# Two batches inside the fourth query slot and a router on the turned residual

## The chip, the cores and the metric

The kernel runs on one core of a Trainium2 chip. The metric is the device time of one execution in microseconds; less is better. Times are compared between medians of several executions.

## What is computed

The reference runs two model blocks over 256 tokens of width 1024, all in float32. The first block has two layers. Each mixes the tokens (a gated linear recurrence in layer 0, stick-breaking attention in layer 1), then looks up rows of a large table (PEER), then adds a gated embedding:

```python
h = h + peer_ffn(rms_norm(h, norm_ffn[i]), peer_w_q[i], peer_sub_keys[i], peer_u[i], peer_v[i])
```

The lookup has 8 heads. For each token and head, 16 of 16,384 rows are picked by two sets of 128 sub-keys; a row of `peer_u` is multiplied with the token, the product goes through gelu and a gate, and scales a row of `peer_v` that is added up. The second block mixes the tokens once more (dilated attention and a chunked recurrence), adds the normed result, and runs a mixture of 32 experts, of which each token uses 4:

```python
x = x + gate_m[:, None, :] * rms_norm_2(y, g_post_mix[l])
h = modulate(rms_norm_2(x, g_pre_ffn[l]), shift_f, scale_f)   # norm * g * (1 + scale) + shift
logits = h @ w_router + b_router
top_val, top_idx = lax.top_k(logits, 4)
gates = jax.nn.softmax(top_val, axis=-1)
act = x_glu * sigmoid(1.702 * x_glu) * (x_lin + 1.0)          # x_glu, x_lin = h @ w_gu[e] + b_gu[e], clipped at 7
y = act @ w_down[e] + b_down[e]
```

## The kernel before

**Layout.** The tokens stand in two tiles of 128 (`t` is 0 or 1). `h` is the residual, `hs` a normed copy, `xT` the turned copy in which the features are on the partitions. PSUM has eight banks: 0 to 2 rotate for projections, 3 is spare, 4 to 7 hold turned tiles, lookup sums or expert outputs. Engines synchronise by counting semaphores, and each engine's instruction stream is written out by hand, in order.

**Lookup layer** (`peer(l, i)` on each engine). The query projection comes in four slots of 512 features. For each slot TensorE projects four quarters (`features`, line 526), ScalarE copies them (line 1189), TensorE multiplies with the sub-keys (line 690), and ScalarE copies the scores (line 1196). VectorE finds the best 16 of each head (`topk`). A pick is one gather on GpSimd's queue (line 2132): 128 rows, one for each token of the tile, each 1024 values of u and 1024 of v, into one of 12 row buffers. There are 256 picks per layer. VectorE multiplies the u half with the token and sums (line 1708). After four picks (a batch) ScalarE applies gelu (line 1154), VectorE the gate (line 1723), ScalarE makes four diagonal matrices (line 1160), and TensorE multiplies them with the v halves into PSUM (`mix_rows`, line 637). Only then, by the semaphore `v_done`, may a new gather overwrite the row buffers. `row_plan` says which buffer each pick uses: eight rotate at first, since four hold the weights of query slots 2 and 3; two join at pick 24 and two at pick 40. Batches 0 and 4 are mixed between the quarters of slot 2, batch 8 behind slot 2's keys, batch 12 behind the second quarter of slot 3, and batch 16 and all later ones behind slot 3. In ScalarE's order the copy of slot 3's first tile stands ahead of batch 12.

**From the output projection to the experts.** `mix_out` is projected in four tiles (lines 541 and 1365 to 1370). VectorE forms the normed, gated result and adds it to `h` (line 1979), squares the residual for its norm, scales it (`scaled`, line 1444), and TensorE turns it (`turn(8, ysb)`, line 557). ScalarE (tile 0) and VectorE (tile 1) copy the turned tile with gain and shift into `xT`. TensorE multiplies with the router's weights `wr`, once for each tile (line 980), and adds the router's bias (line 982). VectorE meanwhile writes the normed rows `hs` with gain (`row_g`) and shift (`row_s`), and clears the buffers `G4`, `Y`, `SGT`, `E` (line 1998). Behind the logits it finds the four best experts of each token (`member`). TensorE counts the tokens of each expert (line 989) and ranks them (991 to 993), and each expert gets blocks of 64 tokens. TensorE gathers the first block's tokens by a one-hot product (`gather`, line 963), turns ranks, gates and rows, and makes tables of experts and ranks for all blocks (lines 1014 to 1020). The product of the gates with the down bias `bdn` starts the output banks 4 to 7 (line 1025).

**Expert loop.** One pass for each block, with a number of passes that is read from memory. A pass starts the gate and up banks with the bias (line 1045), multiplies with eight quarters of weights (line 1051), scatters the block before into the output banks (line 1032), gathers the next block's tokens, and multiplies with four down quarters (line 1077). SyncE loads the weights, 12 MB for an expert, into 12 slots of 1 MB; an expert's first slot is loaded when the last block of the expert before has freed it (`w_free`). GpSimd tells TensorE that a slot's weights are in (`w_here`). After the loop the last block is scattered (line 1032), and the two tiles are normed and stored.

## Time and profile before

| what | value |
|---|---|
| median of 3 runs | 2931.41 us (2931.3 to 2933.35) |
| profiled execution, its own time | 2923.44 us |
| its span, first to last instruction | 2921.3 us |
| busy in the span | TensorE 80%, VectorE 47%, ScalarE 21%, GpSimd 20% |
| mean granted TensorE clock | 0.893 |
| read from HBM | 1047.72 MB, 359 GB/s over the span |

### The profile page before, as it was taken

How to read it: one execution, taken by the hardware profiler on the slowest of the kernel's cores; microseconds unless marked ns; L12 is line 12 of the kernel's file. 1: busy time of each engine (PE TensorE's matmuls, PEld its weight loads, DVE VectorE, ACT ScalarE, POOL GpSimd, SP SyncE). 2: the span in 40 equal slices, each digit the busy share in tenths (PEclk: the TensorE clock that was granted, in tenths of full speed). 3: DMA queues.
4: the chain of work that ended last, by engine and by line, in shares of the span. 5: the costliest groups of instructions: out<-in, count | busy, mean ns of one | idle time of the engine just before them, and what ended most of it. 6: DMA issues, size and time to landing. Idle time of an engine off the chain costs nothing.

```text
span 2921.3 us, 32802 instructions
## 1 busy us (share of the span) xinstructions
PE 2330.0 (80%) x11754; PEld 1004.1 (34%) x11754; DVE 1379.4 (47%) x3401; ACT 604.1 (21%) x1254; POOL 576.7 (20%) x526
## 2 busy tenths in 40 slices
PE   8975556656699975555655699899999999999998
PEld 7741111211165741111211166543333332333333
DVE  5757777776526767777776532521111111111111
ACT  3122212222125112222232121211111111111111
POOL 0034444444300135444444200000000000000000
PEclk9997766887799987777888799889999999999999
DMA  5899999999854899999999743449999999899897
GB/s 220 320 381 422 421 421 421 421 421 421 340 241 159 320 372 419 421 421 421 421 421 418 329 150 116 184 173 387 422 422 422 422 422 422 351 422 422 368 411 293
DMA packets 145310, 1050.19 MB, mean 359 GB/s; under 512 B 16273, under 2 KB 16529, under 8 KB 17969
## 3 DMA queue, kind: packets, MB, share of 16 engines
q0 software_dynamic: 74064, 537.56, 44.6%
q1 hardware_dynamic: 70560, 509.12, 42.7%
q10 hardware_dynamic: 576, 2.16, 0.2%
q8 instruction: 57, 0.93, 0.1%
q14 instruction: 53, 0.43, 0.0%
HBM read 1047.72 MB, written 1.05 MB: 359 GB/s over the span
## 4 chain that ended last, share of the span: by engine, by line
PE 45%; DMA 40%; DVE 5%; POOL 4%; issue 3%; ACT 3%; DVEq 1%; SPq 0%; POOLq 0%
DMA big<-in_peer_uv,rows_of 26%; DMA big<-in_moe 14%; PE psum L1051 11%; PE psum L637 6%; PE psum L526 6%; PE psum L1077 5%; PE psum L541 5%; POOL big L2132 4%; DVE big L1708 2%; PE psum L963 1%; PE psum L1032 1%; PE psum L745 1%; PE psum L654 1%; ACT gdiag L1160 1%; PE psum L1045 1%
## 5 line engine op out<-in xcount | busy, mean ns | idle before, releaser
L637 PE MATMUL psum<-big,gdiag 64*64 64x512 f32 x3728 | 695.3, 847 | 498.2 <-ACT gdiag L1160 498.1
L2132 POOL DMA_INDIRECT big<-in_peer_uv,rows_of x466 | 524.2, 1125 | 1067.9 <-PE psum L637 607.1
L637 PEld LDWEIGHTS psum<-big,gdiag 64*64 64x64 f32 x3728 | 196.0, 189 | 987.2 <-ACT gdiag L1160 603.1
L1051 PE MATMUL psum<-big 128*64 128x512 f32 x2240 | 500.7, 596 | 24.0 <-POOLq L2154 23.3
L1708 DVE CUSTOM_DVE_ANT_0 big<-x_more,big 128x1024 f32<-128x1024 f32 x234 | 286.4, 1226 | 148.9 <-DMA big<-in_peer_uv,rows_of 142.5
L1708 DVE CUSTOM_DVE_ANT_0 big<-mod_rows,big 128x1024 f32<-128x1024 f32 x232 | 284.5, 1227 | 135.1 <-DMA big<-in_peer_uv,rows_of 129.6
L2093 DVE TENSOR_SCALAR big<-psum 128x512 f32<-128x512 f32 x35 | 24.2, 692 | 662.4 <-PE psum L1051 662.4
L1051 PEld LDWEIGHTS psum<-big 128*64 128x64 f32 x2240 | 152.8, 137 | 369.4 <-issue 272.8
L1077 PE MATMUL psum<-ring,big 128*64 128x512 f32 x1120 | 248.0, 594 | 3.7
L1154 ACT ACTIVATE gelu<-dots,rstd 128x4 f32<-128x4 f32 (+1 forms) x134 | 39.8, 297 | 864.8 <-DVE dots L1708 864.7
L526 PE MATMUL psum<-big,ring 128*128 128x256 f32 x832 | 183.3, 380 | 0.8 <-DVE big L1466 0.8
L526 PEld LDWEIGHTS psum<-big,ring 128*128 128x128 f32 x832 | 156.9, 190 | 23.7 <-DVE big L1466 1.2
L541 PE MATMUL psum<-ring,big 128*128 128x512 f32 x352 | 154.2, 595 | 2.7 <-DVE big L1543 1.4
L1160 ACT ACTIVATE gdiag<-small,gated 128x64 f32<-128x64 f32 x512 | 136.9, 336 | 52.9 <-DVE gated L1723 52.1
L1077 PEld LDWEIGHTS psum<-ring,big 128*64 128x64 f32 x1120 | 92.5, 137 | 136.7 <-issue 132.3
L1398 ACT ACTIVATE big<-big 128x512 f32<-128x512 f32 x35 | 22.0, 630 | 487.0 <-DVE big L2093 487.0
L637 PE MATMUL psum<-uv_more,gdiag 64*64 64x512 f32 x368 | 107.3, 709 | 0.0
L541 PEld LDWEIGHTS psum<-ring,big 128*128 128x128 f32 x352 | 66.1, 190 | 83.3 <-issue 78.4
L1032 PE MATMUL psum<-big 64*128 64x512 f32 x288 | 71.5, 615 | 0.7 <-ACT big L1406 0.7
L963 PE MATMUL psum<-big 128*64 128x512 f32 x288 | 71.5, 618 | 0.0
L1406 ACT ACTIVATE big<-psum 128x512 f32<-128x512 f32 x35 | 20.9, 597 | 230.9 <-PE psum L1077 230.9
L1723 DVE SCALAR_TENSOR_TENSOR gated<-gelu,gsum,gexp 128x4 f32<-128x4 f32 (+1 forms) x134 | 29.3, 219 | 67.7 <-ACT gelu L1154 65.3
(394 smaller groups left out, 2142.8 us busy)
## 6 DMA issues: line engine op xcount, KB each, us to landing
big<-in_moe SPq DMA_DIRECT2D x256, 1024.0 KB, 20.1
ring<-in_moe SPq DMA_DIRECT2D x128, 1024.0 KB, 18.9
big<-in_ada SPq DMA_DIRECT2D x24, 1024.0 KB, 11.7
ring<-in_mix_in SPq DMA_DIRECT2D x14, 1024.0 KB, 7.0
ring<-in_a_in SPq DMA_DIRECT2D x8, 1024.0 KB, 8.5
ring<-in_peer_wq SPq DMA_DIRECT2D x8, 1024.0 KB, 7.8
big<-in_peer_wq SPq DMA_DIRECT2D x8, 1024.0 KB, 6.6
ring<-in_ple_gate SPq DMA_DIRECT2D x8, 1024.0 KB, 14.7
```

Of the source, the lines that this page charges most:

```text
L526: mm = pe.matmul(psum[:, (m + t) % 3, f * T:(f + 1) * T], ws[k][:, c:c + P], rhs[:, k, :], start=(k == 0), stop=(k == KC - 1))
L541: mm = pe.matmul(psum[:, (m + t) % 3, :], lhs[:, k, t * P:(t + 1) * P], w[:, k, :], start=(k == 0), stop=(k == KC - 1))
L637: mm = pe.matmul(psum[o:o + HALF, bank, :], gdiag[r:r + HALF, (n + j) % DIAGS, :], v[r:r + HALF, :], start=(at == 0), stop=last, skip_grou ...
L963: mm = pe.matmul(psum[CAP * c:CAP * (c + 1), 2, :], S[:, t, :], hs[:, t, c * 512:(c + 1) * 512], start=(t == 0), stop=(t == TT - 1), skip_ ...
L1032: mm = pe.matmul(psum[:, 4 + 2 * t + c, :], SGT[r, t * P:(t + 1) * P], Y[r, :], start=False, stop=stop, skip_group_check=True)
L1051: mm = pe.matmul(psum[CAP * c:CAP * (c + 1), b, :], xgT[:, k % 4, k // 4, :], wring[k][:, (2 * b + c) * 512:(2 * b + c + 1) * 512], start= ...
L1077: mm = pe.matmul(psum[CAP * c:CAP * (c + 1), 2, :], actT[:, j, f * CAP:(f + 1) * CAP], wring[8 + j][:, (2 * f + c) * 512:(2 * f + c + 1) * ...
L1154: act.activation(gelu[:, cols], dots[:, cols], ACT.Gelu_apprx_tanh, scale=rstd[:, t:t + 1]).then_inc(gelu_ready, 1)
L1160: act.activation(gdiag[:, n % DIAGS, :], ident2, ACT.Copy, scale=gated[:, n:n + 1]).then_inc(gdiag_ready, 1)
L1708: j = dve.tensor_tensor_reduce(out=u, in0=x, in1=u, scale=1.0, scalar=0.0, op0=ALU.mult, op1=ALU.add, accum_out=dots[:, n:n + 1])
L1723: dve.scalar_tensor_tensor(gated[:, cols], gelu[:, cols], total, gexp[:, cols], ALU.mult, ALU.mult).then_inc(gated_act, 1)
L2132: pool.indirect_dma_start(uv[r], None, table, bass.IndirectOffsetOnAxis(rows_of[:, n:n + 1], 0)).then_inc(uv_loaded[r], 16)
```

## The change

Four things are changed.

1. In query slot 3, batch 12 is mixed behind the first quarter and batch 16 behind the third (before: batch 12 behind the second quarter, batch 16 after the slot). ScalarE takes each batch ahead of a tile copy.
2. The router works on the turned residual `h` with the gain only. The inverse root, a factor per token, is applied to the logits afterwards, and the shift's contribution with the router's bias is made once as a row (`logit_bias`). The second tile is turned in two halves, each as soon as its half of `h` is written. The additions of `row_s` are moved: tile 0's ahead of the logits, tile 1's behind `member`.
3. The buffers are cleared before the output projection's tiles come. The output banks are started by `scatter(start=True)`, a product of cleared buffers, behind the logits. The product with `bdn` stands behind the loop, before the last scatter.
4. Order: the first gather stands ahead of the rank turns; gates are formed ahead of the block selection; the register with the number of blocks is loaded earlier on TensorE; the wait for the turned rows stands behind the bias products in the loop; GpSimd signals the first expert's weights before it waits for the table.

```diff
-                inside = {2: {0: 0, 2: BATCH}, 3: {1: 3 * BATCH}}
+                inside = {2: {0: 0, 2: BATCH}, 3: {0: 3 * BATCH, 2: 4 * BATCH}}
...
                     for g in range(2):
+                        if s == 3:
+                            batch((12, 16)[g])
                         act.activation(qT[:, 4 * s + 2 * g:4 * s + 2 * g + 2, :], two(tile_in(m + g)),
                                        ACT.Copy).then_inc(act_took, 1)
...
-                        if s == 3 and g == 0:
-                            batch(12)
...
-            turn(8, ysb)
+            def turn_half(t, b):
+                pe.wait_ge(hs_ready, 17 + t + t * b)
+                for k in range(4):
+                    c = (4 * b + k) * P
+                    mm = pe.transpose(psum[:, 4 + 2 * t + b, k * P:(k + 1) * P], h[:, t, c:c + P], ident)
+                mm.then_inc(turned, 1)
+
+            turn_half(0, 0)
+            turn_half(0, 1)
+            pe.wait_ge(moe_loaded, 160)
+            m = tile0("mix_out") + 1
+            pe.wait_ge(dve_took, TILE_NTH[m])
+            for k in range(KC):
+                pe.matmul(psum[:, m % 3, 0:E2], shift_f[:, k:k + 1].to_broadcast([P, P]), wr[:, k, :],
+                          start=(k == 0), stop=False)
+            pe.matmul(psum[:, m % 3, 0:E2], late[0:1, C_ONES:C_ONES + P], br[0:1, :],
+                      start=False, stop=True).then_inc(row_done, 1)
+            turn_half(1, 0)
+            turn_half(1, 1)
...
             for t in range(TT):
+                pe.wait_ge(xT_ready, 38 + t)
                 if t:
-                    pe.wait_ge(gains_known, 3)
+                    pe.wait_ge(gains_known, 2)
...
+            def scatter(start=False, stop=False):
+                for t in range(TT):
+                    for c in range(2):
+                        r = slice(CAP * c, CAP * (c + 1))
+                        mm = pe.matmul(psum[:, 4 + 2 * t + c, :], SGT[r, t * P:(t + 1) * P], Y[r, :],
+                                       start=start, stop=stop, skip_group_check=True)
+                    if stop:
+                        mm.then_inc(moe_done, 1)
+
+            pe.wait_ge(E_ready, 1)
+            scatter(start=True)
...
             pe.wait_ge(first_ready, 1)
+            gather()
             for t in range(TT):
                 mm = pe.transpose(psum[0:E2, 1, t * P:(t + 1) * P], rank[:, t, :], ident)
             mm.then_inc(rankT_done, 1)
-            gather()
             pe.wait_ge(g_ready, 1)
...
+            n = pe.value_load(blocks[0:1, 0:1], min_val=E2, max_val=BLOCKS - 1)
             turn_rows(1)
...
             with pe.Fori(0, n) as i:
                 pe.wait_ge(E_ready, i + 1)
-                pe.wait_ge(x_taken, i + 1)
                 pe.wait_ge(sgt_taken, i + 1)
...
+                pe.wait_ge(x_taken, i + 1)
                 for k in range(KC):
...
+            for t in range(TT):
+                for c in range(2):
+                    r = slice(E2 * (2 * t + c), E2 * (2 * t + c + 1))
+                    pe.matmul(psum[:, 4 + 2 * t + c, :], gT4[r, :], bdn[r, :], start=False, stop=False,
+                              skip_group_check=True)
             pe.wait_ge(out_taken, n + 1)
-            scatter(True)
+            scatter(stop=True)
```

ScalarE and VectorE at the router, and GpSimd:

```diff
+            def take_half(t, b):
+                act.wait_ge(turned, 32 + 2 * t + b + 1)
                 for k in range(4 * b, 4 * b + 4):
-                    j = act.activation(xT[:, k, 0:P], psum[:, 4 + b, (k % 4) * P:(k % 4 + 1) * P], ACT.Identity,
-                                       scale=gf[:, k:k + 1], bias=shift_f[:, k:k + 1])
+                    j = act.activation(xT[:, k, t * P:(t + 1) * P], psum[:, 4 + 2 * t + b, (k % 4) * P:(k % 4 + 1) * P],
+                                       ACT.Copy, scale=gf[:, k:k + 1])
                 j.then_inc(xT_ready, 1)
+
+            take_half(0, 0)
+            take_half(0, 1)
+            act.wait_ge(row_done, 11)
+            act.activation(logit_bias, psum[:, (m + 1) % 3, 0:E2], ACT.Copy).then_inc(row_taken, 1)
             root(19, 1)
+            take_half(1, 0)
...
+            for r in (G4, Y, SGT, region(12184, 64), E, tk4):
+                dve.memset(r, 3.0e38 if r is tk4 else 0.0)
+            dve.drain()
+            for g in range(4):
+                dve.memset(E[E2 * g:E2 * g + 1, :], 1.0)
+            dve.tensor_copy(ident4[0:E2], ident[0:E2, 0:E2].unsqueeze(1).to_broadcast([E2, 4, E2]))
+            dve.drain().then_inc(E_ready, 1)
             m = tile0("mix_out")
...
+                        for half in range(2):
+                            o = slice(half * 512, (half + 1) * 512)
+                            dve.scalar_tensor_tensor(h[:, t, o], ysb[:, t, o], rstd[:, t:t + 1], h[:, t, o], ALU.mult,
+                                                     ALU.add).then_inc(hs_ready, 1)
                     dve.drain()
                     square(t, h[:, t, :])
+                    if t:
+                        dve.wait_ge(turned, 36)
+                        dve.tensor_tensor(xT[:, 4:8, P:T], psum[:, 7, :].rearrange("p (a b) -> p a b", a=4),
+                                          wide(gf[:, 4:8], P), ALU.mult).then_inc(gains_known, 1)
                     inverse(17 + 2 * t, t)
-                    scaled(t, ysb)
...
+                    dve.wait_ge(row_taken, 10)
+                    dve.scalar_tensor_tensor(hs[:, t, :], h[:, t, :], rstd[:, t:t + 1], row_g, ALU.mult, ALU.mult)
+            dve.drain()
+            dve.tensor_tensor(hs[:, 0, :], hs[:, 0, :], row_s, ALU.add)
...
-            dve.tensor_copy(logit, psum[:, 3, 0:2 * E2].rearrange("p (a b) -> p a b", a=2))
+            for t in range(TT):
+                dve.scalar_tensor_tensor(logit[:, t, :], psum[:, 3, t * E2:(t + 1) * E2], rstd[:, t:t + 1],
+                                         logit_bias, ALU.mult, ALU.add)
...
             dve.drain().then_inc(member_ready, 1)
+            dve.tensor_tensor(hs[:, 1, :], hs[:, 1, :], row_s, ALU.add)
...
-            pool.wait_ge(cell_ready, 1)
-            n = pool.value_load(blocks[0:1, 0:1], min_val=E2, max_val=BLOCKS - 1)
             for r in range(HALVES):
                 pool.wait_ge(w_loaded[r], 16)
                 pool.sem_inc(w_here, 1)
+            pool.wait_ge(cell_ready, 1)
+            n = pool.value_load(blocks[0:1, 0:1], min_val=E2, max_val=BLOCKS - 1)
```

## Rows read from the trace of the kernel before

**Rows 1.** The profile's page: shares of the ending chain, and one costly group.

```profile
PE 45%; DMA 40%; DVE 5%; POOL 4%; issue 3%; ACT 3%; DVEq 1%; SPq 0%; POOLq 0%
...
L1051 PE MATMUL psum<-big 128*64 128x512 f32 x2240 | 500.7, 596 | 24.0 <-POOLq L2154 23.3
```

**Rows 2.** Stretches: length, busy PE PEld DVE ACT POOL, clock, DMA share, GB/s.

```profile
240.00:780.00 540.00, 319.19 (x1756) 93.80 (x1760) 383.02 (x962) 119.81 (x318) 236.63 (x216) 0.76 1.01 421
```

**Rows 3.** Stretches around query slot 3, layer 0 and layer 1.

```profile
184.00:220.00 36.00, 26.00 (x160) 16.06 (x162) 20.01 (x58) 9.24 (x22) 16.32 (x12) 0.94 0.97 375
...
192.00:196.00 4.00, 4.00 (x31) 2.04 (x24) 3.74 (x13) 0.00 (x0) 2.65 (x2) 1.00 0.75 268
...
1060.00:1100.00 40.00, 28.75 (x176) 14.89 (x178) 24.98 (x69) 10.60 (x27) 18.63 (x14) 0.87 0.97 374
```

**Rows 4.** Order of time around slot 3, layer 0: start, us, engine, instruction [idle].

```profile
181.90 7.17 PE L526 MATMUL psum<-big 128*128 128x256 f32 x32
...
183.84 1.23 DVE L1708 CUSTOM_DVE_ANT_0 big<-mod_rows,big 128x1024 f32<-128x1024 f32 x1
...
190.82 3.66 PE L637 MATMUL psum<-big,gdiag 64*64 64x512 f32 x32 [1.75 <-ACT gdiag L1160]
...
193.04 1.61 POOL L2132 DMA_INDIRECT big<-in_peer_uv,rows_of  x1 [5.92 <-PE psum L637]
...
196.74 1.94 POOL L2132 DMA_INDIRECT big<-in_peer_uv,rows_of  x1 [0.30 <-issue]
...
209.12 3.96 PE L637 MATMUL psum<-big,gdiag 64*64 64x512 f32 x18 [3.01 <-ACT gdiag L1160]
...
212.94 0.94 POOL L2132 DMA_INDIRECT big<-in_peer_uv,rows_of  x1 [10.54 <-PE psum L637]
```

**Rows 5.** Order of time, layer 1: the two mixes.

```profile
1063.42 3.66 PE L637 MATMUL psum<-big,gdiag 64*64 64x512 f32 x32 [1.75 <-ACT gdiag L1160]
...
1081.72 2.70 PE L637 MATMUL psum<-big,gdiag 64*64 64x512 f32 x16 [3.01 <-ACT gdiag L1160]
```

**Rows 6.** Order of time from the output projection to the logits.

```profile
1869.06 0.69 DVE L1972 TENSOR_TENSOR big<-psum,uv_more 128x512 f32<-128x512 f32 x1 [8.04 <-ACT big L1365]
...
1890.97 2.89 ACT L1375 ACTIVATE big<-psum,modv,tiny 128x128 f32<-128x128 f32 x8
...
1891.34 1.28 DVE L1979 SCALAR_TENSOR_TENSOR h<-big,rstd,h 128x1024 f32<-128x1024 f32 x1
...
1895.52 1.97 PE L557 MATMUL psum<-small,big 128*128 128x128 f32 x8 [5.70 <-DVE big L1444]
...
1901.24 3.62 PE L980 MATMUL psum<-big 128*128 128x32 f32 x16
...
1902.92 1.15 DVE L1998 MEMSET big<- 128x128 f32 x6
```

**Rows 7.** The stretch of the router's preparation, same columns as rows 2.

```profile
1897.00:1915.00 18.00, 15.50 (x67) 11.30 (x65) 12.84 (x55) 0.96 (x3) 0.00 (x0) 0.50 0.00 0
```

**Rows 8.** Order of time from the counts to the loop.

```profile
1907.24 0.53 PE L989 MATMUL psum<-big 128*32 128x48 f32 x4 [1.82 <-DVEq L2020]
...
1910.30 0.61 PE L1002 MATMUL psum<-small,big 128*32 128x128 f32 x2 [0.68 <-DVEq L2038]
...
1910.84 3.68 PE L963 MATMUL psum<-big 128*64 128x512 f32 x8
...
1917.84 1.14 PE L1025 MATMUL psum<-big 32*128 32x512 f32 x8
...
1919.93 13.95 PE L1051 MATMUL psum<-big 128*64 128x512 f32 x64
```

**Rows 9.** Order of time in the last passes and behind the loop.

```profile
2870.84 1.94 PE L963 MATMUL psum<-big 128*64 128x512 f32 x8
...
2881.26 1.09 PE L1045 MATMUL psum<-big 32*64 32x512 f32 x8
...
2909.26 1.99 PE L1032 MATMUL psum<-big 64*128 64x512 f32 x8 [0.69 <-ACT big L1406]
```

More of the change, by code:

```diff
@@ L313, in build @@
         G = region(11680, TT, E2)
+        logit_bias = scratch[:, 0:E2]
         logit = region(11744, TT, E2)
@@ L710, in project @@
                     mm.then_inc(prod_done, 1)
-                for n in range(4 * BATCH, PICKS):
+                for n in range(5 * BATCH, PICKS):
                     if n == 148:
@@ L1021, in _ @@
                       start=True, stop=True).then_inc(table_done, 1)
-            for t in range(TT):
-                for c in range(2):
-                    r = slice(E2 * (2 * t + c), E2 * (2 * t + c + 1))
-                    pe.matmul(psum[:, 4 + 2 * t + c, :], gT4[r, :], bdn[r, :], start=True, stop=False,
-                              skip_group_check=True)
-            def scatter(stop):
-                for t in range(TT):
-                    for c in range(2):
-                        r = slice(CAP * c, CAP * (c + 1))
-                        mm = pe.matmul(psum[:, 4 + 2 * t + c, :], SGT[r, t * P:(t + 1) * P], Y[r, :],
-                                       start=False, stop=stop, skip_group_check=True)
-                    if stop:
-                        mm.then_inc(moe_done, 1)
-            n = pe.value_load(blocks[0:1, 0:1], min_val=E2, max_val=BLOCKS - 1)
             with pe.Fori(0, n) as i:
                 pe.wait_ge(E_ready, i + 1)
-                pe.wait_ge(x_taken, i + 1)
                 pe.wait_ge(sgt_taken, i + 1)
@@ L1058, in _ @@
                 pe.wait_ge(out_taken, i + 1)
-                scatter(False)
+                scatter()
                 pe.wait_ge(S_ready, i + 1)
@@ L1206, in peer @@
                             continue
-                        if at >= 16:
+                        if at >= 20:
                             batch(at, size)
@@ L1978, in _ @@
                     inverse(16 + 2 * t, t)
-                    dve.scalar_tensor_tensor(h[:, t, :], ysb[:, t, :], rstd[:, t:t + 1], h[:, t, :], ALU.mult, ALU.add)
+                    if t == 0:
+                        dve.scalar_tensor_tensor(h[:, t, :], ysb[:, t, :], rstd[:, t:t + 1], h[:, t, :], ALU.mult,
+                                                 ALU.add).then_inc(hs_ready, 1)
+                    else:
+                        for half in range(2):
+                            o = slice(half * 512, (half + 1) * 512)
+                            dve.scalar_tensor_tensor(h[:, t, o], ysb[:, t, o], rstd[:, t:t + 1], h[:, t, o], ALU.mult,
+                                                     ALU.add).then_inc(hs_ready, 1)
@@ L1986, in _ @@
-            for b in range(2):
-                dve.wait_ge(turned, 34 + b + 1)
-                for k in range(4 * b, 4 * b + 4):
-                    j = dve.tensor_scalar(xT[:, k, P:T], psum[:, 6 + b, (k % 4) * P:(k % 4 + 1) * P], gf[:, k:k + 1],
-                                          shift_f[:, k:k + 1], ALU.mult, ALU.add)
-                j.then_inc(gains_known, 1)
-            for t in range(1, TT):
-                dve.scalar_tensor_tensor(hs[:, t, :], h[:, t, :], rstd[:, t:t + 1], row_g, ALU.mult, ALU.mult)
+                    dve.wait_ge(row_taken, 10)
@@ L1994, in _ @@
+                    dve.scalar_tensor_tensor(hs[:, t, :], h[:, t, :], rstd[:, t:t + 1], row_g, ALU.mult, ALU.mult)
             dve.drain()
+            dve.tensor_tensor(hs[:, 0, :], hs[:, 0, :], row_s, ALU.add)
+            dve.wait_ge(row_taken, 11)
+            dve.wait_ge(logits_done, 1)
             for t in range(TT):
-                dve.tensor_tensor(hs[:, t, :], hs[:, t, :], row_s, ALU.add)
-            for r in (G4, Y, SGT, region(12184, 64), E, tk4):
-                dve.memset(r, 3.0e38 if r is tk4 else 0.0)
@@ L2064, in _ @@
             dve.drain().then_inc(g_ready, 1)
+            dve.tensor_tensor(rs[0:E2, :], nth[0:E2, :], nb[0:E2, :], ALU.is_lt)
+            dve.drain()
+            dve.scalar_tensor_tensor(sel[0:E2, :], nth[0:E2, :], -0.5, rs[0:E2, :], ALU.is_gt, ALU.mult)
+            dve.drain()
+            dve.scalar_tensor_tensor(rs[0:E2, :], sel[0:E2, :], -float(CAP), nth[0:E2, :], ALU.mult, ALU.mult)
+            dve.wait_ge(rankT_done, 1)
+            dve.tensor_copy(rankT[0:E2, :], psum[0:E2, 1, 0:T])
+            dve.drain().then_inc(sel_ready, 1)
             dve.wait_ge(table_done, 1)
```

36 lines of the change are left out of this document (6 added, 30 removed).

## Prediction

> **What bounds the kernel now.** I read the chain that ended last first, then the stretches, then the order of time in the three places that the diff touches. The chain is almost all TensorE and DMA [rows 1]. The stretches say which of them counts where. Through the steady part of a lookup layer DMA is full at 421 GB/s while TensorE is busy 319 of 540 us [rows 2]: a gather is 128 rows of 8 KB, 1.05 MB, and so takes 2.49 us, and the layer ends when its 256 gathers have come through. So nothing that TensorE does there counts, except where it leaves DMA short of work. It does so while the last two query slots are projected: 375 and 374 GB/s over 36 and 40 us, and 268 GB/s in the worst 4 us [rows 3]. The router's preparation is the opposite: nothing moves on DMA and TensorE runs at 0.50 of its clock (1.2 GHz) [rows 7], and each engine waits for another. The expert loop follows; the loads for the second expert wait for the slots that its first pass frees, so the whole loop, DMA included, moves with its start.
>
> The profiled execution took 2923.44 us, 2.1 us more than its span and 0.27% under the median of 2931.41. I take the sum off 2923.44 and move the same difference to the median.
>
> **Part 1, two batches inside slot 3.** Now slot 3's four quarters surround one mix of four picks. The picks' dot products are there early: the read at 183.84 is the last of batch 12 and ends at about 185.1, but ScalarE can't start on it, since its queue first holds the copy of a tile that is finished at 189.1 (181.90 + 7.17). So the mix starts at 190.82 and the next gathers at 193.04; batch 16 is mixed only behind slot 3, the keys and the exponents, at 209.12, and frees rows from 212.94 [rows 4]. With eight to ten rows in rotation that is why DMA runs dry. After the change ScalarE takes batch 12 at 185.1, in front of the tile: gelu, gates and diagonals take 1.7 us here (189.1 to 190.82), so the mix starts at about 186.8 instead of 190.8, and gather 20 at about 189 instead of 193. Quarter two ends at 186.8 + 3.66 + 3.6 = 194.1, quarter three at 197.7; batch 16 (its rows have landed: gathers 16 to 19 are issued by 187.1, which is 193.04 less the wait of 5.92, and the last of them is in by about 195) is mixed there, 11 us earlier than at 209.12. Slot 3 itself ends some 3 us later (one mix more, 3.66, less the idle 1.75 of before, plus a wait of about 1 for the diagonals); behind it wait keys, the turned-back rows of tile 1 and the exponents for picks from 32 on, none needed before pick 32 is read. Gathers 26 to 29 are issued from 199.9, while 20 to 25, six of 2.49 us behind 195, keep DMA busy to about 209.
>
> What this is worth is DMA's shortfall: (421 - 375) / 421 x 36 = 3.9 us in layer 0 and (421 - 374) / 421 x 40 = 4.5 us in layer 1, whose mixes at 1063.42 and 1081.72 stand in the same pattern [rows 3, 5]. All of it, 8.4 us, is the upper bound. The part that is surely a late release is the hole of 192 to 196, (421 - 268) / 421 x 4 = 1.45 us, once in each layer: 2.9 us is the lower bound. The rest has a second reason: gather issues stretch from 0.94 to 1.94 us beside Vector's products [rows 4]. Between the bounds I take the middle, **5.7 us**. Zero is excluded only if the next release comes in time, as worked out above.
> The Trainium skill, SBUF — State Buffer, section "SBUF: two separate sides", calls the port that Vector and GpSimd share an exclusive lock, whose loser blocks for the whole instruction. By the rows an issue costs at most 1.94 + 0.30 = 2.24 us, under a gather's 2.49; by that rule it may cost 0.94 + 1.23 + 0.30 = 2.47, no backlog builds, and the sum of this part would be 2.9 (the third rival).
>
> **Part 2, the router on the turned residual.** Before: the second tile's residual is updated from 1891.34, squared, rooted, scaled, and only then turned at 1895.52; TensorE has idled 5.70 us, works at half clock, turns for 2 us and runs both tiles' logits, the second from 1901.24, free at 1905.42 (1.82 us before 1907.24) [rows 6 to 8]. The inverse root goes behind the router now, since it is one factor per token, and the shift's contribution becomes one row of 18 tiny matmuls, placed between the two tiles' turns, where TensorE waits anyway. New order: turn tile 0, bias row (to about 1891.8 at full clock), turn tile 1 by halves from 1892.1 to 1893.4. ScalarE's eight copies end at 1890.97 + 2.89 = 1893.9; logits of one tile take 3.4 us at half clock (the 3.62 less the last product's way out) or 1.7 at full. Then the bias row's copy, the root and four more copies (0.2 + 0.2 + 1.45): 1895.9. Second tile: 1897.7 at full clock. Vector does the other half (0.69), keeps 1.28 for the rows and as much for the added shift: 1891.34 + 1.28 + 1.4 + 0.7 + 0.3 + 2.6 = 1897.6, just in time. The clearing (1.15 us and small things, under 2.5 in all) stood on Vector before the logits and now lies in its 8.04 us wait under the output projection [rows 6]; there it costs nothing, and left where it was it would cost its 2.5.
>
> From the free TensorE to the counts: 1.82 before, 1.95 now (two scaled additions for one copy). In this gap stands the new clearing of the four output banks by a product of zeros, eight 64-row passes like the last scatter's, 1.99 us at full clock [rows 9] and about 3.6 at half. Counts to the first one-hot: 3.06 before (1907.24 to 1910.30); the addition to tile 1's rows (1.28 at most) runs while TensorE counts (0.53) and ranks; it makes the block numbers some 0.6 later and finds the ranks already there, so I add 0.2 (0.7 at most). One-hot to the loop's first weights product: 9.63 before (1910.30 to 1919.93) [rows 8]. Off it come the rank turns ahead of the gather (0.54), the gather's half clock (3.68 to 1.94, [rows 8, 9]) and the output bias (1.07 of its 1.14); the register load moves ahead of the row turns and costs 0.7 there: 9.63 - 0.54 - 1.74 - (1.07 - 0.7) = 7.0. For that GpSimd's twelve signals that the first expert's weights are in must not wait for the expert table, and they are moved ahead of that wait; left behind it they would take the 1.07 back. The loads of the router's weights, for which TensorE now waits before tile 1's turns, are issued before the projection starts, some 27 us earlier.
> - Full clock throughout: 1897.7 + 1.95 + 3.25 + 7.0 = 1909.9, **10.0 us** earlier than 1919.93.
> - Half clock from 1893 on: logits to 1900.7, clearing to 1904.3, then 3.06 + 8.75: 1916.1, **3.8 us** earlier.
>
> Which? Small products don't raise a fallen clock: from 1897 to 1915 TensorE was busy 15.5 of 18 us and the granted clock stayed 0.50 [rows 7]. Whether they keep up one that hasn't fallen, the trace doesn't show. There are pauses of 0.5 us where 5.7 was, but also 3.5 us of thin work between clearing and gather. I take the middle, **7.0**.
> The Trainium skill, TensorE: Matmul & The Clock Gate, section "Why this matters for your kernels", asks only that pauses between products be short; by that the clock would hold and this part would give the 10.0 of the full-clock line, by the row above less.
>
> **Behind the loop.** The output bias, eight 32-row passes, starts when the last down product is done; the last scatter waited 0.69 us there for ScalarE's copy, and such passes take 1.09 [rows 9]. 1.09 - 0.69 = **+0.4 us** (0 if they overlap wholly). The wait for x moved behind the bias products changes nothing: its copy is long done.
>
> **Sum.** -5.7 - 7.0 + 0.4 = -12.3. 2923.4 becomes 2911.1; the median 2931.4 becomes **2919**.
>
> **Rivals.**
> - Forecast, both parts near the middle: 2919, 42%.
> - The clock holds: for it speak the short pauses, against it the row of 18 us. -5.7 - 10.0 + 0.4: 2916 (2913 with all of DMA's shortfall), 22%.
> - The gathers' issues hold DMA back: for it the stretched 1.94, against it that the steady part runs at 421 with the same products beside. -2.9 - 7.0 + 0.4: 2922, 14%.
> - The clock is gone from 1893: -5.7 - 3.8 + 0.4: 2922; with the former too, 2925, 10%.
> - Nearly nothing arrives: DMA's holes return at the next batches, since the exponents for picks 32 on and their table loads merely move behind batch 16, and the clock is low: -3.8 + 0.4: 2928, within the bound, 7%.
> - Slower: the logits are now summed in another order (factor and shift behind the sum). If that turns one token's fourth choice at an expert that holds exactly 64 or 65 tokens, there are 36 or 34 blocks for 35 (2240 products at 64 a block, [rows 1]). One more costs a pass, 2909.26 - 2881.26 less the wait 0.69, 27.3 us: 2946. It needs a near tie at just that border, 3%; 2% more for what I don't see.
>
> A difference under 0.2% (5.9 us) is not told from none in this kernel. Faster: 42 + 22 + 14 + 10 = 88, less what falls inside the bound by chance, 87; same 8; slower 5. Range 2910 to 2927: from the clock held with all of DMA's shortfall, less the spread of the runs, to both low bounds.
>
> **What would show it.** Slot 3's two mixes near 186.8 and 197.7, no 4 us under 350 GB/s between 190 and 220, and the layer's last gather some 3 us earlier, twice. TensorE's turns of tile 1 near 1892.5 less 6, no idle 5.70, and a granted clock that tells which of 7.0's ends it is; the loop's first product 6 to 10 us earlier relative to the projection's end. The last scatter 1.0 instead of 0.69 behind the last down product. I am wrong if DMA's shortfall reappears after 220, if the counts wait for the clearing products, or if the loop has another number of passes.

## The result and the profile after

The changed kernel takes 2912.79 us, the kernel before 2931.3 us, medians of five runs each (2911.07 to 2916.7 and 2925.97 to 2933.35). The medians are 18.5 us apart. The ratio, taken over all runs, is 0.9943 with a 95% interval of 0.9933 to 0.9954, so by it the change is worth 16.7 us, between 13.5 and 19.6. The forecast was 2919, from 2910 to 2927. The number of passes is unchanged (2240 products, below, as in [rows 1]).

The profile's page of the changed kernel, chain and loop product:

```profile
PE 44%; DMA 40%; DVE 5%; POOL 4%; ACT 2%; issue 2%; DVEq 1%; SPq 0%; POOLq 0%
...
L1064 PE MATMUL psum<-big 128*64 128x512 f32 x2240 | 500.6, 596 | 24.5 <-POOLq L2183 23.9
```

Stretches around slot 3 (columns of [rows 2]), to be read beside [rows 3]:

```profile
184.00:220.00 36.00, 29.20 (x184) 18.17 (x180) 24.12 (x70) 9.35 (x22) 16.15 (x14) 0.96 0.96 383
192.00:196.00 4.00, 4.00 (x25) 2.65 (x18) 1.91 (x6) 0.00 (x0) 3.39 (x3) 1.00 0.98 391
184.00:186.00 2.00, 2.00 (x19) 0.86 (x12) 1.89 (x5) 0.00 (x0) 1.22 (x2) 1.00 0.23 94
1060.00:1100.00 40.00, 30.13 (x200) 16.52 (x200) 25.41 (x68) 10.25 (x26) 18.77 (x17) 0.96 1.01 414
```

In layer 1 the 374 GB/s have become 414. In layer 0 the hole of 192 to 196 is gone (391 for 268), but a hole ahead of it, 94 GB/s behind batch 8, has stayed: over the 8 us from 50 us after the first gather on, DMA moved 301 GB/s before (180 to 188) and 281 after (182 to 190). This trace starts its gathers 1.96 us later than the one of before. The order of time shows the same (layer 0, and two lines of layer 1), as in [rows 4, 5]:

```profile
184.48 0.94 POOL L2161 DMA_INDIRECT big<-in_peer_uv,rows_of  x1 [7.88 <-PE psum L638]
...
189.60 3.66 PE L638 MATMUL psum<-big,gdiag 64*64 64x512 f32 x32 [0.53 <-ACT gdiag L1178]
...
191.81 0.94 POOL L2161 DMA_INDIRECT big<-in_peer_uv,rows_of  x1 [1.44 <-PE psum L638]
...
200.85 0.30 ACT L1172 ACTIVATE gelu<-dots,rstd 128x4 f32<-128x4 f32 x1 [3.30 <-DVE dots L1732]
...
202.25 2.36 PE L638 MATMUL psum<-big,gdiag 64*64 64x512 f32 x18 [1.89 <-ACT gdiag L1178]
...
204.47 0.93 POOL L2161 DMA_INDIRECT big<-in_peer_uv,rows_of  x1 [4.10 <-PE psum L638]
...
217.10 5.36 PE L638 MATMUL psum<-big,gdiag 64*64 64x512 f32 x32 [3.01 <-ACT gdiag L1178]
...
220.96 1.45 POOL L2161 DMA_INDIRECT big<-in_peer_uv,rows_of  x1 [11.45 <-PE psum L638]
...
1060.48 3.66 PE L638 MATMUL psum<-big,gdiag 64*64 64x512 f32 x32 [0.53 <-ACT gdiag L1178]
1072.98 2.36 PE L638 MATMUL psum<-big,gdiag 64*64 64x512 f32 x18 [1.73 <-ACT gdiag L1178]
```

The gathers are numbered from 0, as the picks are. Gather 20 waits 1.44 us for its row and no longer 5.92, gather 26 waits 4.10 for 10.54; the mix of batch 16 still waits 1.89 us for ScalarE, which waits for the dot products. The wait that still costs transfer time is the first line: 7.88 us, in front of gather 16, for the mix of batch 8. The longest wait, 11.45 us in front of gather 30, costs none, since enough gathers are under way: from 218 to 230 DMA moved 418 GB/s.

The router in order of time, beside [rows 6, 8]; the projection ends at 1884.43 (1888.21 before):

```profile
1855.51 1.15 DVE L1991 MEMSET big<- 128x128 f32 x6
...
1887.19 2.15 ACT L1394 ACTIVATE big<-psum,tiny 128x128 f32<-128x128 f32 x8
...
1888.36 1.32 PE L963 MATMUL psum<-small,h 128*128 128x128 f32 x8 [0.43 <-DVE h L2016]
...
1889.52 6.64 PE L998 MATMUL psum<-big 128*128 128x32 f32 x32
...
1896.09 3.79 PE L1006 MATMUL psum<-big 64*128 64x512 f32 x8
...
1899.81 0.44 PE L1017 MATMUL psum<-big 128*32 128x48 f32 x4
...
1902.27 1.94 PE L983 MATMUL psum<-big 128*64 128x512 f32 x8 [0.75 <-DVEq L2067]
...
1907.61 1.09 PE L1057 MATMUL psum<-big 32*64 32x512 f32 x8
1908.62 1.94 PE L1064 MATMUL psum<-big 128*64 128x512 f32 x8
```

The projection's end is here the start of its last group of products. The idle 5.70 us has become 0.43. From the projection's end to the loop's first product it is 24.19 us (31.73 before). Stretches of the same part, beside [rows 7]:

```profile
1884.00:1889.80 5.80, 5.37 (x41) 4.45 (x39) 4.58 (x9) 3.04 (x12) 0.00 (x0) 1.00 0.60 225
1890.00:1896.00 6.00, 6.00 (x29) 6.00 (x29) 3.67 (x7) 2.52 (x6) 0.00 (x0) 0.50 0.29 122
1896.00:1899.80 3.80, 3.80 (x9) 1.21 (x9) 2.77 (x12) 0.53 (x2) 0.00 (x0) 0.50 0.00 0
1900.00:1902.00 2.00, 1.38 (x16) 1.10 (x14) 1.24 (x7) 0.00 (x0) 0.00 (x0) 1.00 0.00 0
```

So neither end of the forecast came about alone: the clock fell to 0.50 (1.2 GHz) as the logits began, although TensorE had not paused for more than 0.5 us since the projection, and was back at 2.4 GHz for the gather. Behind the loop, beside [rows 9]:

```profile
2897.67 1.14 PE L1097 MATMUL psum<-big 32*128 32x512 f32 x8
...
2898.74 1.99 PE L1006 MATMUL psum<-big 64*128 64x512 f32 x8
```

### The profile page after: what moved, and what is told of

It reads as the page before. It is cut to its first block, busy times and chain, and to the rows that moved or that the text cites. A ratio compares the mean times of both kernels' runs of the same rounds, so it can differ in the third digit from the quotient of the medians.

```text
span 2910.8 us, 32845 instructions
## 1 busy us (share of the span) xinstructions
PE 2330.9 (80%) x11776; PEld 1004.7 (35%) x11776; DVE 1376.1 (47%) x3394; ACT 604.3 (21%) x1258; POOL 567.0 (19%) x526
## 4 chain that ended last, share of the span: by engine, by line
PE 44%; DMA 40%; DVE 5%; POOL 4%; ACT 2%; issue 2%; DVEq 1%; SPq 0%; POOLq 0%
DMA big<-in_peer_uv,rows_of 25%; DMA big<-in_moe 14%; PE psum L1064 11%; PE psum L638 7%; PE psum L527 6%; PE psum L1090 5%; POOL big L2161 4%; PE psum L542 4%; DVE big L1732 2%; PE psum L1006 1%; PE psum L983 1%; PE psum L655 1%; PE psum L746 1%; ACT gdiag L1178 1%; PE psum L1057 1%
## 5 line engine op out<-in xcount | busy, mean ns | idle before, releaser
L2161 POOL DMA_INDIRECT big<-in_peer_uv,rows_of x466 | 513.6, 1102 | 1072.2 <-PE psum L638 612.1
L1064 PE MATMUL psum<-big 128*64 128x512 f32 x2240 | 500.6, 596 | 24.5 <-POOLq L2183 23.9
L2122 DVE TENSOR_SCALAR big<-psum 128x512 f32<-128x512 f32 x35 | 24.2, 691 | 658.8 <-PE psum L1064 658.8
L527 PE MATMUL psum<-big 128*128 128x256 f32 x256 | 58.3, 383 | 0.0
```

The costliest lines, as they stand in the source:

```text
L527: mm = pe.matmul(psum[:, (m + t) % 3, f * T:(f + 1) * T], ws[k][:, c:c + P], rhs[:, k, :], start=(k == 0), stop=(k == KC - 1))
L1064: mm = pe.matmul(psum[CAP * c:CAP * (c + 1), b, :], xgT[:, k % 4, k // 4, :], wring[k][:, (2 * b + c) * 512:(2 * b + c + 1) * 512], start= ...
L2161: pool.indirect_dma_start(uv[r], None, table, bass.IndirectOffsetOnAxis(rows_of[:, n:n + 1], 0)).then_inc(uv_loaded[r], 16)
```

## The experiments

Each kernel was timed in five rounds beside the kernel before, 5 to 11 runs each; the lengths come from one profiled run of each. All lengths in this table are differences of start times in the order of time and rounded: the gathers of both layers (first to last issue, summed), the output projection (its first product to the start of its last group), from there to the loop's first weights product, and from the last down product to the end. "us" is the median; the ratio stands with its interval.

| kernel | gathers | projection | to the loop | behind | us | ratio |
|---|---|---|---|---|---|---|
| before | 1299.8 | 27.1 | 31.7 | 13.3 | 2931.3 | 1 |
| changed | 1292.7 | 28.8 | 24.2 | 13.6 | 2912.8 | 0.9943 (0.9933 to 0.9954) |
| slot 3 alone | 1292.1 | 29.3 | 33.2 | 13.3 | 2921.9 | 0.9968 (0.9955 to 0.9980) |
| router alone | 1300.1 | 29.3 | 25.0 | 13.6 | 2922.2 | 0.9962 (0.9950 to 0.9975) |
| clearing uncovered | 1293.9 | 29.3 | 25.4 | 13.6 | 2914.8 | 0.9942 (0.9929 to 0.9955) |
| bias in front | 1292.8 | 28.8 | 25.3 | 13.3 | 2912.9 | 0.9945 (0.9933 to 0.9958) |
| batch 12 only | 1299.4 | 29.2 | 25.0 | 13.7 | 2926.6 | 0.9980 (0.9971 to 0.9988) |
| clearing in logits | 1293.0 | 29.4 | 33.6 | 13.6 | 2925.2 | 0.9969 (0.9958 to 0.9981) |
| clearing behind gather | 1294.7 | 29.3 | 26.1 | 13.6 | 2917.4 | 0.9950 (0.9937 to 0.9962) |
| batch 8 in slot 2 | 1287.2 | 29.3 | 25.0 | 13.6 | 2909.4 | 0.9929 (0.9916 to 0.9941) |
| signals behind | 1291.1 | 29.2 | 25.0 | 13.6 | 2913.5 | 0.9945 (0.9927 to 0.9962) |
| batch 16 only | 1296.8 | 27.1 | 23.5 | 13.6 | 2915.2 | 0.9954 (0.9941 to 0.9967) |
| batch 8, clearing split | 1289.4 | 27.1 | 23.5 | 13.6 | 2912.1 | 0.9940 (0.9927 to 0.9953) |
| changed again | 1293.9 | 28.9 | 24.2 | 13.6 | 2914.5 | 0.9948 (0.9934 to 0.9961) |

The projection's code is the same in all of them, and yet takes 27.1, 28.8 or 29.3 us: the granted clock is at 0.50 for none, the first 3.5 or the first 4.3 to 4.5 us of it. What follows behind it goes with this. So router times are compared at the same projection: 31.7 to 23.5 at 27.1 (before, batch 16 only), and 33.2 to 25.0 at 29.3 (slot 3 alone, router alone). Both say **8.2 us**, but in different parts. At 27.1 the counts start 6.9 us earlier (19.0 to 12.1 us after the projection's end), with the gather at half clock in both. At 29.3 they start only 4.1 earlier (19.0 to 14.9), and the rest comes behind them: the gather runs at full clock in place of half, 1.94 us for 3.68, and of the two bias products ahead of the loop, 1.9 us each at half clock in this pair, one is gone. That both sums are 8.2 is in part chance.

Stretches that the edits leave alone differ between the profiles too: from the last gather to the projection it is 206.4 to 211.8 us, between the two layers' gathers 221.7 to 226.2, and in the loop, where only the place of a wait differs, 987.9 to 990.1. Where medians and the lengths in the table disagree by a few us, this is as large.

**Slot 3 alone.** The kernel before with the first of the four changes only.

> The kernel before with nothing but the two batches inside slot 3. If DMA's shortfall in both layers is what the second batch gives back, as forecast: -5.7 us, 2925.7 us, with gather 26 some 8 to 12 us earlier after gather 20 in both layers, and the first-to-last-gather times 3 us shorter in each. Rival (what the one profile of the changed kernel suggests): a gain of about 7 us in layer 1 and none in layer 0, so -7, because in layer 0 the batches ahead of slot 3 leave a hole of their own. Rival 2, the late release only costs where DMA actually stands still (1.45 us a layer): -2.9. Rival 3: no gain at all, everything comes from the router; then 2931.

The gain is 0.32% or 9.4 us (5.9 to 13.2) by the median, and 7.7 us over both layers by the trace, 2.4 in layer 0 and 5.3 in layer 1. No gain at all is ruled out, and so is the lower bound by the interval. Over the eight profiles with both batches in slot 3 and batch 8 behind slot 2, the gathers take 1293.0 us on average (1291.1 to 1294.7), over the two with the old slot 1299.8 and 1300.1: 6.9 us.

**Router alone.** The changed kernel with the old slot 3.

> The changed kernel with slot 3 as it was before (one batch inside it), so the router, the clearing and the output bias are changed alone. By the forecast's terms -7.0 + 0.4 = -6.6 us, 2924.8. By the change measured between the two profiles (projection's end to first loop product -7.53, loop +0.47, behind the loop +0.33) -6.7. If the sum of the two parts is more than the whole (they overlap or collide), it is nearer to -12 here; if part 1 gives everything, 0.

0.38% or 11.1 us (7.3 to 14.7), and by the trace 8.2 less 0.3 behind the loop. The interval just reaches down to the 7.9 of the trace. The two parts add up within their intervals. They are tested as wholes: which of the router's edits (the root behind the logits, the turns by halves, the order) gives how much of it is only read from the trace.

**Batch 12 first, batch 16 behind.** The changed kernel with this, and ScalarE's and TensorE's orders to match:

```diff
-                inside = {..., 3: {0: 3 * BATCH, 2: 4 * BATCH}}
+                inside = {..., 3: {0: 3 * BATCH}}
```

> The changed kernel with batch 12 moved to slot 3's first quarter, and batch 16 mixed behind the slot again, as before. Theory A, the second batch inside the slot is the one that frees rows in time: gather 20 stays at 60 us after the layer's first (59.8 in the changed kernel, 63.0 to 64.4 with the old slot), gather 26 goes back from 72 to 80 or later, and most of the 7 us that part 1 gave over both layers is lost: +5, 2918. Theory B, the hole of 192 to 196 us in front of gather 20 was the loss, and batch 12 alone closes it: gather 26 later without effect, 2913 to 2914.

Theory A: the gathers are back at 1299.4 us. A stretch and the gather that ends it:

```profile
214.00:218.00 4.00, 3.37 (x20) 0.74 (x12) 3.70 (x9) 0.00 (x0) 2.83 (x2) 0.68 0.45 139
```

```profile
214.86 1.88 POOL L2161 DMA_INDIRECT big<-in_peer_uv,rows_of  x1 [14.79 <-PE psum L638]
```

The hole in front of gather 20 is closed, and a new one of 139 GB/s stands 20 us later, where the next release is late by 14.79 us. To fill one hole only moved it: alone, batch 12's place is worth nothing that these traces can tell (1299.4 for 1299.8 and 1300.1). The median of 2926.6 is 8.6 us above what was expected, and 4.4 above that of the router alone, from which only this edit separates it. In the profiles that difference stands in the untouched stretches (4.3 us more between the layers and ahead of the projection), and the intervals of the two ratios still meet.

**Batch 16 added, batch 12 in its old place.** `3: {1: 3 * BATCH, 2: 4 * BATCH}`.

> The changed kernel with batch 12 left behind slot 3's second quarter, as before, and batch 16 added behind its third. Theory A (the second batch carries part 1, the place of the first is worth nothing): gather 20 late as before (63 to 64 us after the layer's first), gather 26 at about 74, median within 2 us of the changed kernel, 2912 to 2915. Theory B (both places matter because a late batch 12 makes batch 16 late too): half of part 1 lost, 2916 to 2917.

The trace stands between the theories: 1296.8 us, outside the 1291.1 to 1294.7 of the kernels with both edits, and 3.2 of the 6.9 us, with gather 20 at 64.2 us and gather 26 at 74.0 after the layer's first (59.8 and 72.5 in the changed kernel). The medians, 2915.2 and 2914.5 on the same chip, don't tell them apart. The second batch is needed, and gives its full worth only with the first one early.

**A step further: batch 8 ahead of slot 2's keys.** The calls behind the keys are taken out.

```diff
+                    if s == 2:
+                        mix_early(2 * BATCH)
                     pe.wait_ge(act_took, TILE_NTH[m - 1])
...
+                        if s == 2 and g == 1:
+                            batch(8)
                         act.activation(qT[:, 4 * s + 2 * g:4 * s + 2 * g + 2, :], two(tile_in(m + g)),
```

> A step further on part 1: batch 8 mixed before slot 2's keys and not behind them, ScalarE's share of it in front of the slot's second copy. Theory A, what is left of DMA's shortfall is the late release of batch 8's rows (the hole from 184 to 190 us in layer 0, some 2.5 to 4 us in each layer): gather 16 issued at 48 us after the first in place of 52.5, both layers 2 to 4 us shorter, 2906 to 2909. Theory B, the shortfall only moves on to the next wait (batch 12's dot products end at 56.3 whatever happens): 2912 to 2913. Theory C: slot 2's keys come later and with them the exponents, which picks from 20 on need: slower, 2915.

Gather 16 is issued 48.1 us after the layer's first (52.5 in the changed kernel), and the gathers take 1287.2 us, 5.9 less than the average of the changed forms. The 26 us from 44.1 us after the first gather on, in the changed kernel and then in this one:

```profile
176.00:202.00 26.00, 21.40 (x134) 13.83 (x133) 15.67 (x46) 5.68 (x17) 12.62 (x11) 1.00 0.92 354
```

```profile
174.00:200.00 26.00, 23.71 (x146) 14.61 (x148) 17.76 (x49) 6.05 (x18) 13.34 (x12) 0.93 0.97 385
```

(421 - 354) / 421 x 26 = 4.1 us were missing there, now 2.2 (layer 0). The median is 2909.4, the lowest of all, 0.71% under before. Its interval still meets that of the changed kernel (0.9916 to 0.9941 against 0.9933 to 0.9954), so the gain over the changed kernel is shown by the gathers' times and only likely by the medians. The second kernel with this edit ("batch 8, clearing split") has 1289.4 us, 3.6 less than the average, and a median of 2912.1 beside 2914.5 for the changed kernel on the same chip. The average of the two is 4.7 us less.

**Clearing uncovered.** Vector's clearing back in front of its wait for the logits.

> The changed kernel with Vector's clearing of the buffers put back behind the residual's work, just ahead of its wait for the logits. As forecast (uncovered it costs its 2.5 us): 2915.3, and the counts 2.5 us later after the projection's end. Rival, from the profile after, where Vector is idle for 2.4 us ahead of the logits anyway: it fits there, and the zero products that wait for the cleared buffers start when the logits end or 0.3 us behind: 2912.8 to 2913.1.

```profile
1893.24 6.27 PE L998 MATMUL psum<-big 128*128 128x32 f32 x32
...
1897.59 1.15 DVE L2025 MEMSET big<- 128x128 f32 x6
...
1899.76 3.79 PE L1006 MATMUL psum<-big 64*128 64x512 f32 x8 [0.25 <-DVEq L2030]
```

The rival is right. The clearing takes 2.2 us (1897.59 to 1899.76), nearly all of it while TensorE is still at the logits, and TensorE waits 0.25 us for it. The counts start 15.3 us after the projection's end; in the kernels with the same projection time and the clearing in its new place it is 15.0.

**Output bias in front of the loop.**

> The changed kernel with the output bias product back in front of the expert loop. As forecast the bias costs its 1.07 us in front and 0.4 behind, where ScalarE's copy covers the rest, so +0.67 us: 2913.5, with the last scatter 1.0 us earlier behind the last down product by at most 0.4. Rival 1: the loop's own start is set by the first expert's other waits (x, tables) and not by TensorE's queue, so the product in front is covered and the move behind only cost: -0.3, 2912.5. Rival 2: the bias behind the loop is wholly hidden: +1.1.

```profile
1906.19 1.14 PE L1054 MATMUL psum<-big 32*128 32x512 f32 x8
1907.26 1.09 PE L1062 MATMUL psum<-big 32*64 32x512 f32 x8
...
2897.93 1.99 PE L1006 MATMUL psum<-big 64*128 64x512 f32 x8 [0.69 <-ACT big L1430]
```

To the loop 25.27 us in place of 24.19 at the same clock (+1.08), behind it 13.33 in place of 13.65 (-0.32): the move is worth 0.76 us (forecast 0.67), too little for the medians.

**Signals behind the table's wait.** GpSimd's twelve `sem_inc(w_here, 1)` put back.

> The changed kernel with GpSimd's twelve signals for the first expert's weights put back behind its wait for the expert table. As forecast that takes 1.07 us back: the loop's first weights product starts 25.3 us after the projection's end where the same clock gave 24.2 (or 26.1 where the dips of the clock gave 25.0), 2913.9. Rival: what ends last ahead of that product is TensorE's own bias product or the x copy, and the signals come in time: no change, 2912.8.

```profile
1909.30 1.98 PE L1057 MATMUL psum<-big 32*64 32x512 f32 x8
...
1911.22 2.08 PE L1064 MATMUL psum<-big 128*64 128x512 f32 x6
```

The weights product follows the bias product without a pause, 25.01 us behind the projection's end, exactly as in the two kernels with the signals ahead and the same clock (25.02 and 25.01: router alone, batch 8 in slot 2). The bias product is at half clock here. In the kernel before, where the signals are behind as well and the clock is full, the first weights product follows the loop's bias product by 1.02 us, after the change by 1.01. The signals' place costs nothing.

**Clearing between the logits.** A zero product behind the second and the sixth product of each tile's logits.

> The changed kernel with the four zero products (512 columns wide) placed between the thin logit products instead of behind them. Theory A, width keeps the clock: the logits' clock stays at 1.00 longer than 0.3 us into them, the logits with the clearing take 5.3 to 6.5 us in place of 10.4, counts start 1.6 us or more before their 15.4 us after the projection's end, 2909 to 2911. Theory B, the clock falls at its moment whatever is issued: the sum of both stays about 10.3 us, only Vector's reading of the logits starts later (its 1.5 us then run behind all of it), counts 1.5 to 2 us later, 2914.5.

```profile
1891.92 1.84 PE L1004 MATMUL psum<-big 64*128 64x512 f32 x2
1893.69 1.92 PE L999 MATMUL psum<-big 128*128 128x32 f32 x8
1895.54 2.07 PE L1004 MATMUL psum<-big 64*128 64x512 f32 x2
```

Both theories fail: logits and clearing take 14.9 us and not 10.4 or less, and the loop starts at 33.6. The clock fell at the same place and stayed at 0.50 for 23.9 us, to 0.9 us behind the gather. Each zero product alone takes 1.84 to 2.07 us, while four in a row take 3.79, 0.95 each. Such a product uses one half of the rows, and its neighbour the other half; the times fit two of them running beside each other when they follow each other. The eight runs of this kernel fall into two groups, three from 2916.7 to 2919.6 us and five from 2924.9 to 2927.6; the profile is of the second, and what the clock does in the first wasn't traced.

**Clearing behind the gather.**

> The changed kernel with the zero products behind the one-hot gather and the rank turns. Counts then wait only for Vector: 13.8 us after the projection's end in place of 15.4. Theory A, the wide zero products are what brings the clock back: it is still 0.50 in the gather, which takes 3.7 us in place of 1.94, and the loop starts 0.5 to 1.5 us later than the changed kernel's 24.2: 2914. Theory B, the clock returns by itself: gather at full clock, 1.6 earlier, zero products cost about 1 us of it again: loop starts 0.5 us earlier, 2912.5.

```profile
1898.84 0.53 PE L1014 MATMUL psum<-big 128*32 128x48 f32 x4 [2.08 <-DVEq L2047]
...
1902.00 3.36 PE L983 MATMUL psum<-big 128*64 128x512 f32 x8 [0.61 <-DVEq L2066]
...
1905.61 1.99 PE L1006 MATMUL psum<-big 64*128 64x512 f32 x8
```

Theory A. The counts now wait only for Vector and start 13.4 us after the projection's end in place of 15.0 (clearing in its place, same projection). But the gather comes at half clock, 3.36 us for 1.94, and the zero products delay what follows: 26.1 to the loop for 25.0. So the zero products in front of the counts cost 1.6 us and here pay it back.

**Batch 8 in slot 2, clearing split.** Two zero products before the logits, two behind.

> Batch 8 moved into slot 2 as in the last kernel but one, and the zero products split: tile 0's two (they share TensorE, one on each half of the rows) before the logits, where the clock is still full, tile 1's two behind them. Theory A, four wide products in a row are what brings the clock back: with two the clock is still 0.50 in the gather, which takes 3.4 to 3.7 us, and the loop starts 25.5 to 26.5 us after the projection's end in place of 25.0: 2910.5. Theory B, width doesn't matter or two are enough: counts 0.7 us earlier, gather 1.94, loop start 24.3, 2908.7.

The clock in this kernel went the third way (projection 27.1), in which the logits run at full clock. Both theories took the clock to be low there, so neither is tested. The kernel is compared with the kernel with batch 16 only, which has the clearing in one piece:

```profile
1890.53 1.87 PE L998 MATMUL psum<-big 128*128 128x32 f32 x16
1892.90 1.97 PE L998 MATMUL psum<-big 128*128 128x32 f32 x16 [0.50 <-ACT big L1396]
...
1894.80 2.83 PE L1006 MATMUL psum<-big 64*128 64x512 f32 x8
...
1900.62 3.68 PE L983 MATMUL psum<-big 128*64 128x512 f32 x8 [0.68 <-DVEq L2069]
```

The counts start 12.1 us after the projection's end in both, the gather is at half clock in both, the loop starts at 23.5 in both. Splitting gives nothing here, and whether two zero products in a row would bring a fallen clock back stays open.

**The changed kernel again.**

> The changed kernel as it is, beside the other three on this chip, to compare them with: 2912.8, the interval of its ratio around 0.9943. Loop start 24.2 or 25.0 us after the projection's end, depending on whether the clock dips between gather and loop.

2914.5 us, ratio 0.9948, 24.2 us to the loop: the profile repeats to 0.1 us in the router, to 1.2 us in the gathers.

## Why the prediction was right, point by point

**Part 1** was forecast at -5.7 and measured at -6.9, within its 2.9 to 8.4. Its mechanism, rows freed in time for DMA, is what the two split kernels show. Its times, as distances from the layer's first gather: mix 12 was to come at 56.8 and came at 57.6, gather 20 at 59.0 and 59.8, mix 16 at 67.7 and 70.3, gather 26 at 69.9 and 72.5. Batch 16 is 2.6 us late because the forecast set it by the quarter's end, and it was its dot products that ended last (ScalarE waits 3.30 us for them at 200.85). Slot 3 starts in the changed profile 1.5 us later after the first gather than before, and layer 0 gave no gain there at all (648.5 in both). Over eight profiles, beside the two with the old slot, it gave 2.3 us and layer 1 gave 4.6; the two old ones differ by as much as that between them (648.5 and 651.1 in layer 0), and only their sums agree. The sub-forecast "3 us earlier, twice" held only as an average. What the forecast did not see is where the rest stays: behind batch 8, ahead of slot 3. The two kernels with batch 8 in slot 2 get 5.9 and 3.6 us of it.

The third rival, gather issues that hold DMA back, is out: issues are as long as before (the longest takes 1.99 us in the trace of before and in every other), and DMA fills anyway, at 412 GB/s from 190 to 220 in the changed kernel.

**Part 2** was forecast at -7.0 between 3.8 and 10.0, and measured at -8.2, at the same projection. The step that failed is the picture of the clock as one of two ends. It fell in the logits and came back ahead of the gather, or held through the logits and was gone in the gather; 24.2, 25.0 and 23.5 us are so near to each other because one loss stands for the other. The middle of two lines, neither of which came about, is no mechanism, and that it lay within 1.2 us is partly luck. Priced with the forecast's own terms, the course that the clock took in the changed kernel is: logits at half clock done 12.5 us after the projection's end, clearing 3.6, from the counts to the gather 3.25, from the gather on 7.0 at full clock, together 26.3 us to the loop, or 5.4 earlier than before. It took 24.2: 11.7, then 3.6, 2.5 and 6.35. So three terms were too long, by 0.8, 0.8 and 0.65. The logits came early because the eight copies without a shift took 2.15 us and not 2.89. From the counts to the gather the forecast took the 3.06 of before, measured at half clock, for both lines, with 0.2 on top in the full one; at full clock it is 2.5 (1899.81 to 1902.27), at half clock 3.06 without the 0.2 (batch 16 only). With the logits at full clock the first term was right (9.5 forecast, 9.43 in the kernel with batch 16 only), and with a half-clock gather the last took 8.30 for 8.75.

"Small products don't raise a fallen clock" was read from 1897 to 1915 of before. That stretch also holds the 512-wide gather (1910.84 to 1914.5), and in the 2 us behind it the mean clock is 0.84: it came back there, and not while the thin products before the gather ran.

The Trainium skill, TensorE: Matmul & The Clock Gate, section "Why this matters for your kernels", asks only for short pauses to keep a clock that is up. By that the clock would have held; this trace does not agree: it has 0.50 from 1890 to 1896 with TensorE busy 6.00 of 6.00 us, so here short pauses were not enough.

**The clearing** was said to be worth 2.5 us through its cover. That was wrong: it is 0.3 us, since Vector waits for the logits anyway. Nothing hung on it in the sum. **The signals** were said to be worth 1.07 us; they are worth nothing. The gain of 1.07 in front is the output bias's own, and 1.08 was measured. **Behind the loop**: forecast +0.4, measured +0.32.

**Sum.** Forecast -12.3; by the traces -6.9 - 8.2 + 0.3 = -14.8, with the router at the same projection and the gathers averaged; by the ratio -16.7 (13.5 to 19.6) and in the repeat 0.52%, -15.2. The one pair of profiles, before and changed, is only 10.5 us apart (spans of 2921.3 and 2910.8): gathers -7.1 and router -7.5, but the first gather comes 2.0 us later, the projection takes 1.7 longer, the loop 0.5 and the end 0.3, and the profiled run of before was 8 us faster than its median. The median of 2912.8 lies where the rival "the clock holds" was put (2916 or 2913), but its mechanism did not occur. The counts did wait for the clearing, 1.6 us, which the forecast had named as a way to be wrong; its half-clock line held that wait already. The slower rival needed another number of passes, and there were 35 in every profile (2240 products).

## What to carry to other kernels

Where one transfer engine is the bound and its buffers are freed by a batch of work, look at all late releases in a row: here filling one hole moved the shortfall to the next, and one of the two edits alone measured as nothing. When a forecast lies between two courses, price the course that came about before calling the forecast good. Before a move is credited with hiding something, look whether the engine that did it was waiting there anyway. And compare a stretch at half and full clock only with profiles in which the same code ahead of it took the same time.

## What the runs showed of the hardware

- The granted clock fell in the router 5.3 to 5.9 us after the projection's end in every profile whose projection took 28.8 us or more, the one with the old router (slot 3 alone, TensorE idle there) among them, and 10.4 us after it in the two of the new router with 27.1; the kernel before, with 27.1 as well, has it at 3.5. What set these moments wasn't traced further.
- In each it came back near the end of an unbroken row of 512-wide products, from 0.5 us before it to 1.7 us behind: the clearing (3.79 us at half clock) or the gather (3.36 to 3.68 us). Thin products, and wide ones strewn among thin ones (13.30 us busy of 15.00 at 0.50, in the kernel with the clearing between the logits), were not followed by it. With the clearing behind the gather it stayed down for 13.7 us in place of 10.2. Whether the width is the cause isn't shown.
- Two float32 products of 64 rows, one on each half of the rows, take 0.95 us each in a row of four and 1.84 to 2.07 alone, at half clock, as if two ran beside each other.
- ScalarE's copy of 128x128 with a scale (`ACT.Copy`) takes 0.27 us (2.15 for eight), with scale and shift (`ACT.Identity`) 0.36 (2.89 for eight, [rows 6]); whether the function or the shift makes the difference isn't separated.
